# Two modulation products of layer 1 computed inside the norm between the layers

## The reference, cut to what matters

```python
def modulation(cond, w_mod, b_mod):            # w_mod: 1024 x 6144
    m = jax.nn.silu(cond) @ w_mod + b_mod
    return jnp.split(m[..., None, :], 6, axis=-1)

for l in range(2):
    mc, ml = modulation(c_ctx, ...), modulation(c, ...)      # context, latent
    hc, hl = modulate(xc, mc[0], mc[1]), modulate(xl, ml[0], ml[1])
    dc, dl = mixer(hc), mixer(hl)                # layer 1: pool_mixer
    x  = layer_norm(ALPHA * x + m[2] * d, ln1)   # m[2]: gate of the mixer
    f  = square(relu(modulate(x, m[3], m[4]) @ w_up)) @ w_down
    x  = layer_norm(ALPHA * x + m[5] * f, ln2)   # m[5]: gate of the MLP

def pool_mixer(h, p):
    u = h @ p["w_in"]                            # 1024 -> 1024
    pooled = multiscale_pool(u)                  # four windows, one per 256 channels
    mixed = einsum(pooled, pool_w) * pool_scale  # four 256x256 products
    return mixed @ p["w_out"]
```

## Time and profile before

| | us |
|---|---|
| median of 3 runs | 1475.55 |
| lowest, highest | 1473.79, 1476.63 |
| the profiled execution, its own time | 1473.62 |
| its span | 1471.8 |
| TensorE busy in it | 1405.8 (96%) |
| mean granted TensorE clock | 0.989 |

### The profile page before, as it was taken

One profiled execution on the slowest core, in us unless ns is written; L12 is line 12 of the kernel. 1 busy time (PEld: TensorE's weight loads), 2 busy tenths in 40 slices (PEclk: granted clock), 3 DMA queues, 4 the chain that ended last, 5 costly groups with the idle time before them and its releaser, 6 DMA issues.

```text
span 1471.8 us, 22812 instructions
## 1 busy us (share of the span) xinstructions
PE 1405.8 (96%) x8806; PEld 1245.6 (85%) x8806; DVE 1039.6 (71%) x1645; ACT 542.7 (37%) x976; POOL 79.1 (5%) x146
## 2 busy tenths in 40 slices
PE   4999999899999999999999999989999999999996
PEld 3899988666788998998899879868999899889985
DVE  3694566677468976776776796757797677667678
ACT  3333353267435432332233244434443233223322
POOL 1300000011200000000000010001000000000001
PEclk8999999999999999999999999999999999999998
DMA  9701233596713322322221523542332232123141
GB/s 317 220 29 59 87 117 129 167 342 209 249 57 114 130 84 61 115 79 65 85 92 58 208 77 129 186 148 76 121 125 84 62 111 85 59 85 98 59 172 72
DMA packets 132300, 177.47 MB, mean 121 GB/s; under 512 B 4170, under 2 KB 104258, under 8 KB 131698
## 3 DMA queue, kind: packets, MB, share of 16 engines
q1 hardware_dynamic: 123250, 146.46, 31.0%
q0 software_dynamic: 7376, 26.76, 5.3%
q10 hardware_dynamic: 1584, 3.01, 0.5%
HBM read 166.94 MB, written 9.27 MB: 120 GB/s over the span
## 4 chain that ended last, share of the span: by engine, by line
PE 80%; DVE 8%; ACT 5%; DMA 3%; issue 2%; ACTq 0%; POOL 0%; SPq 0%; DVEq 0%
PE ps L779 40%; PE ps L1288 20%; PE ps L761 7%; PE ps L770 4%; PE ps L810 2%; DVE convT L1992 2%; PE ps L1105 2%; ACT h_full L1688 1%; DVE wlo L1896 1%; DMA gate_parts<-modrow 1%; ACT whi L1398 1%; ACT tmp L1688 1%; PE ps L1116 1%; ACT e_att L1608 1%; DMA raw<-in_w_mod_l 1%
## 5 line engine op out<-in xcount | busy, mean ns | idle before, releaser
L1398 ACT ACTIVATE whi<-raw 128x512 fp32r<-128x512 f32 (+2 forms) x186 | 175.4, 953 | 357.1 <-PE ps L779 294.0
L779 PE MATMUL ps<-whi,hid_hi 128*128 128x512 f32 x640 | 249.6, 390 | 0.0
L779 PE MATMUL ps<-wlo,hid_hi 128*128 128x512 f32 x640 | 249.2, 389 | 0.0
L779 PE MATMUL ps<-whi,hid_lo 128*128 128x512 f32 x640 | 249.1, 389 | 0.0
L1896 DVE TENSOR_TENSOR wlo<-raw,whi 128x512 fp32r<-128x512 f32 (+2 forms) x186 | 201.7, 1093 | 24.4 <-ACT whi L1398 21.0
L779 PE MATMUL ps<-whi,h_hi 128*128 128x256 f32 (+1 forms) x480 | 158.7, 331 | 8.7 <-DVE h_lo L2696 5.4
L2325 DVE TENSOR_TENSOR acc<-acc,ps 128x512 f32<-128x512 f32 x120 | 80.3, 684 | 122.0 <-PE ps L779 122.0
L779 PE MATMUL ps<-whi,h_lo 128*128 128x256 f32 (+1 forms) x480 | 153.9, 321 | 0.0
L779 PE MATMUL ps<-wlo,h_hi 128*128 128x256 f32 (+1 forms) x480 | 153.7, 320 | 0.0
L779 PEld LDWEIGHTS ps<-whi,hid_hi 128*128 128x128 f32 x640 | 120.1, 188 | 25.3 <-DVE wlo L1896 0.8
L779 PEld LDWEIGHTS ps<-whi,hid_lo 128*128 128x128 f32 x640 | 120.1, 188 | 25.2
(11 more groups left out here) (337 smaller groups left out, 2669.9 us busy)
## 6 DMA issues: line engine op xcount, KB each, us to landing
raw<-in_w_up_l SPq DMA_DIRECT2D x32, 1024.0 KB, 5.6
raw<-in_w_down_l SPq DMA_DIRECT2D x32, 1024.0 KB, 5.1
raw<-in_w_mod_l SPq DMA_DIRECT2D x28, 1024.0 KB, 5.5
raw<-in_w_in_l SPq DMA_DIRECT2D x12, 1024.0 KB, 5.3
raw_split<-in_w_mod_l SPq DMA_DIRECT2D x8, 1024.0 KB, 6.9
raw<-in_w_out_l SPq DMA_DIRECT2D x5, 1024.0 KB, 6.2
x_spill<-x_tok POOLq DMA_DIRECT2D x10, 512.0 KB, 2.9
x_tok<-x_spill POOLq DMA_DIRECT2D x10, 512.0 KB, 6.0
```

What stands on the lines that cost most here:

```text
L779: mm = pe.matmul(out, a_of(still, k), w_of(part, k), start=(first and k == 0 and part == 0 and still == 0), stop=(last and k == nk - 1 and ...
L1398: act.activation(ring_piece(whi, w, g), piece(w, g), ACT.Copy).then_inc(hi_done, 1)
```

## The change

Products 40 and 41 (blocks 8 and 9 of layer 1) leave the loop of pool products and stand between `last_down(0)` and `first_units(1, ...)`. Their PSUM banks are 4 and 5, which groups 6 and 7 of the last down product used; PE waits for `acc_ok` 77 and 78 before them. Block 8 is loaded into slot 4 (the mixer's gate rows, no longer needed) ahead of w_in; block 9 into slot 2 (the first two accumulator tiles), once DVE has folded these into x (`acc_pre` 2), ahead of the second block of w_in. ACT copies the two rows after the second `split_hi` of the norm and stores them after the norm. The clearing of `ub` on POOL moves behind the norm, since block 9 lies in its place; `turn(1, 3)`, which writes banks 4 and 5, waits for both row copies.

The six products left (42 to 47) stand after the pool products f = 0, 1, 2, 3, 4 and 7. The stream has other places and other slots from there on.

```diff
 def weight_stream():
-            s += [("in", 1, BW * j) for j in range(4)] + [("pool", 1, 0)]
-            s += [("mod", 1, b) for b in (8, 9, 10, 11, 20)] + [("out", 1, 0)] + [("mod", 1, b) for b in (21, 22, 23)]
+            s += [("mod", 1, 8), ("in", 1, 0), ("mod", 1, 9)] + [("in", 1, BW * j) for j in range(1, 4)] + [("pool", 1, 0)]
+            s += [("mod", 1, b) for b in (10, 11, 20)] + [("out", 1, 0)] + [("mod", 1, b) for b in (21, 22, 23)]
...
-        OUT_SLOT = dict(zip(range(POOL_K + 1, POOL_K + 13), (3, 4, SOON, LATE, 3, 2, 4, SOON, LATE, 3, SOON, 2)))
+        MIX_K = mod_k[M_TAIL]
+        OUT_SLOT = dict(zip(range(MIX_K, MIX_K + 17), (4, 0, 2, 1, 0, 1, 0, 3, 4, 1, 2, 0, 3, 4, 1, 0, 2)))
...
         def tail_bank(m):
+            if m in (M_TAIL, M_TAIL + 1):
+                return 4 + m - M_TAIL
             return 6 if m > M_TAIL and m % 2 else 7
... SP, load
-                if k == POOL_K + 6:
+                if k == MIX_K + 2:
+                    sp.wait_ge(acc_pre[0], 2)
+                if k == w_k[W_OUT[1]]:
                     sp.wait_ge(pl_lo, KT)
... POOL
-            pool.memset(ub[:], 0.0).then_inc(zeros, 1)
             for g in range(2):
                 pool.dma_start(ic[:, g, :], ...)
             norm_share(1)
+            pool.wait_ge(mod_main, M_TAIL + 2)
+            pool.memset(ub[:], 0.0).then_inc(zeros, 1)
... PE, turn
+                if t == 3 and i == 1:
+                    pe.wait_ge(mod_row, M_TAIL + 2)
... PE, last_down
+                if layer == 0:
+                    for n in range(2):
+                        pe.wait_ge(acc_ok, DOWNS * layer + 77 + n)
+                        mod_product(M_TAIL + n)
... PE, loop of pool products
-                tail_mods(KT + f)
+                if f < 5 or f == 7:
+                    mod_product(M_TAIL + 2 + min(f, 5))
... ACT, last_norms
                 split_hi(w + 1)
+                if i == 1:
+                    mod_rows(M_TAIL)
+                    mod_rows(M_TAIL + 1)
                 normed(i, 3)
... ACT, after last_norms(1, W_IN1)
+            store_rows(M_TAIL)
+            store_rows(M_TAIL + 1)
... ACT, loop of pool products
-                tail_store(KT + f)
+                if 1 <= f < 6:
+                    store_rows(M_TAIL + 1 + f)
                 if f == 6:
                     split_hi(W_OUT[1])
-                tail_rows(KT + f)
+                if f < 5 or f == 7:
+                    mod_rows(M_TAIL + 2 + min(f, 5))
```

More of the change, by code:

```diff
@@ L363, in mlp_steps @@
                 yield kind, n, None
+        SITES = 32
+        M_TAIL = 8 + SITES
         THIRD_K = mod_k[22]
         POOL_K = w_k[W_IN1 + 4]
-        SOON, LATE = POOL_K % 2, (POOL_K + 1) % 2
-        OUT_SLOT = dict(zip(range(POOL_K + 1, POOL_K + 13), (3, 4, SOON, LATE, 3, 2, 4, SOON, LATE, 3, SOON, 2)))
+        MIX_K = mod_k[M_TAIL]
+        OUT_SLOT = dict(zip(range(MIX_K, MIX_K + 17), (4, 0, 2, 1, 0, 1, 0, 3, 4, 1, 2, 0, 3, 4, 1, 0, 2)))
         ATT_SLOT = dict(zip(range(THIRD_K, THIRD_K + 22), (2, 0, 1, 3, 4, 2, 0, 1, 3, 4, 2, 0, 1, 3, 4, 2, 0, 3, 4, 1, 0, 1)))
@@ L380, in raw_block @@
             if k >= FIRST_K and raw_slot(k) == 2:
-                return raw_pool[:] if k >= POOL_K else raw_att[:]
+                return raw_pool[:] if k in OUT_SLOT else raw_att[:]
             if k in ATT_SLOT and raw_slot(k) > 2:
@@ L488, in sums_of @@
             return 4 * (NS_UP * layer + u - SU)
-        SITES = 32
-        M_TAIL = 8 + SITES
         SKIP = 17
@@ L1350, in _ @@
             mlp(0)
[L1353 to L1356, removed]
             first_units(1, W_IN1, half_mm, u_mm)
@@ L1367, in _ @@
                         .then_inc(u_mm, 1)
-                    tail_mods(f)
             w = W_IN1 + 4
@@ L1838, in _ @@
                     split_hi(W_IN1 + (f + 3) // 2)
-                tail_rows(f)
             pool_high(KT - 1)
```

## The result

The changed kernel took 1477.85 us (median of 8 runs, 1476.51 to 1481.43) where the kernel before took 1474.67 (8 runs, 1472.25 to 1476.63). The medians are 3.2 us apart. The ratio estimated from all runs is 1.0028 (95% interval 1.0017 to 1.0039), which is 4.1 us slower, between 2.5 and 5.7. The forecast was 1.6 us faster. Its time lay in the range, its sign was wrong.

The account below looks back on a forecast made before the run. TensorE was taken as the bound, 80% of the chain. Norm +1.59, pool loop -0.35 and clock -2.88 summed to -1.64 us, taking 1475.55 to 1473.9 us; range 1470.8 to 1478.6.

Parts of the forecast that it names:

- Norm, +1.59: Layer 1's norm: the second moved product waits for DVE's read of group 7, so w_in starts 1.59 us late.
- ACT's freed work, -1.05: Pool loop: two row copies and one store leave ACT, gaining 1.05 us before w_out if block 21 is on time.
- Block 21, a stall of 4.1 us: Pool loop: block 21, landing in 8.4 us behind w_out's first block, keeps TensorE waiting 4.1 us after f = 3.
- the sum of this step, -0.35: Pool loop: with ACT's freed work and block 21's stall together, w_out starts 0.35 us earlier.
- The clock: Idle time before w_out: cut from 5.42 to 3.6 us, it no longer drops TensorE's clock; gain 2.88 us.
- the -2.88 of the sum: Start of w_out: 2.88 us gained on its first 48 matmuls because TensorE's clock stays up.
- a rival with a point at 4.3 us: Pool loop: TensorE's wait for block 21 reaches 4.3 us, its clock falls, costing 2.86; sum +2.0 or +4.9; 20%.
- Clock as it was: Before w_out: the clock still drops, or other runs did not lose it; sum +1.24, 1476.8 us; 17%.
- the late block: Pool loop: block 21 lands after 954.4 and the clock falls there; +2.0, 1477.6 us, or +4.9, 1480.4; 20%.
- the sum with both falls (+4.9): Clock falls in the pool loop and before w_out: +4.9 us, 1480.4; a third of a 20% case.

Follow-up runs that it names:

- Bank 3: The changed kernel with product 41 put in PSUM bank 3 in place of bank 5; 1474.78 us, ratio 1.0007.
- both costs mended: The changed kernel with product 41 in PSUM bank 3 and blocks 21 and 22 loaded ahead of w_out's first block; 1471.41 us, ratio 0.9979.
- the filled stall: The changed kernel with 14 matmuls of no use before product 45, where TensorE waits for block 21; 1477.00 us, ratio 1.0017.
- fillers: Useless matmuls in TensorE's idle time: 14 before product 45, changed kernel, 1477.00 us; 20 before w_out, kernel before, 1472.39; 14 there, mended kernel with spare rows, 1467.74.
- spare rows: Two extra row buffers so row copies don't wait for stores: in the kernel before, 1471.33 us; in the kernel with both costs mended, 1468.35 us.

## Why the prediction was wrong, step by step

**Norm, +1.59: right.** The second product ran at 877.30, 0.05 us behind the end of DVE's read of group 7 (876.56 + 0.69); 1.64 us reached the last w_in units. Bank 3 took it away. What hid the rest held too: ACT's two row copies and four stores lie in waits, and the transposes and units kept their distances.

**ACT's freed work, -1.05: right, but it showed only with the stream mended.** The kernel with both costs mended has 58.51 against 59.56. That it agrees to the digit is luck: from the scale of f = 5 on 8.50 us were left of 9.69, which is 1.19, and 0.14 were lost ahead of it. With block 21 alone moved up it was lost again to a store that landed later.

**Block 21, a stall of 4.1 us: right in kind, 3.42 by the landing of 7.8** (8.4 taken), and 4.63 by 9.0 in another execution. Two further kernels with the same stream had 8.3 and 8.4, so the 8.4 was well chosen. Without the clock the sum of this step, -0.35, holds as well: the filled stall gave -0.21. In the sum itself 0.2 us slipped: from the scale of f = 6 to w_out it was 7.05, less 0.45 for the store makes 6.6 and not 6.4. It measured 6.58 (965.99 to 972.57), and the step should have read about -0.2.

**The clock: the step that failed.** It was put as "at 3.6 I take it as held, because that is short of 4.3". The idle time before w_out was 4.03 us rather than 3.6, and the clock fell 3.1 us into it, where 3.6 would have met it too; so the -2.88 of the sum was not gained (+0.12). And the same reading left the clock up in the stall, which I made a rival with a point at 4.3 us. It fell at 2.8 us, in a stall of 3.42. From 955.24 to f = 5's start at 962.05 TensorE took 6.81 us, in the filled kernel 4.09 (958.20 to 962.29): 2.72 lost at the lower clock, near the 2.86 of that rival; less 0.64 by which the block came later in the filled kernel's loop this is the 2.1 between the two loops. That rival's sum was +2.0 with the fall in the loop alone and +4.9 with both; the case came out, with both, at +4.0 in the trace and +4.1 by the ratio (+3.2 by the medians). Of the 5.6 us between the forecast's -1.6 and the trace's +4.0, 3.0 lie at w_out's start and 2.2 in the loop.

What stands in place of "held below 4.3" is a tally of the twelve profiles, over all idle times of TensorE above 0.5 us from 60 us on, up to its last matmul:

| idle time, us | how many | the clock fell behind |
|---|---|---|
| 0.5 to 1.67 | 189 | 0 |
| 1.77 to 1.80 | 13 | 2 |
| 1.84 to 1.87 | 12 | 7 |
| 2.06 to 2.67 | 26 | 18 |
| 3.15 | 1 | 0 |
| 3.42 to 5.61 | 12 | 12 |

The falls came 1.9 to 5.2 us behind the last matmul ahead of the idle time, some of them when PE worked again. One row of one execution can't give the point at which the clock holds. And the trace of the kernel before had more than one row: its clock fell behind the 1.87 us at 1032.33, and behind 2.16 us at 366.51. Both are shorter than the 2.60 that stood for "left the clock up". The forecast had the doubt: the Trainium skill, TensorE: Matmul & The Clock Gate, Part 1, says that the monitor's window runs freely and that a kernel doesn't set its phase. The runs agree with it, by 7.28 against 8.80 us behind the same idle time of one kernel.

The doubt was weighed wrongly. Two idle times of 3.6 and 4.1 us had to keep the clock in most runs; with one observed fall at 4.3 and one hold at 2.60 that was no better than even for each, and both had to hold. "Clock as it was" and the late block together deserved more than 37%, and the sum with both falls (+4.9) no less than that with none.

**Left open.** What sets the moment of a fall. Whether it is the bunched loads that delay the row stores: the distance from a store's issue to the copy that waits for it was 5.57, 5.60 and 5.67 us in the three profiles with the stream of the kernel before, 5.63 to 6.29 in the four with the changed stream (6.29 being 948.50 to 954.79), 6.91 with block 21 moved up and 5.87 with both costs mended; a tendency, with the ranges overlapping. And how much of the medians' difference comes from unit 0: the kernel before dropped its clock there in 3 of the 4 executions with that idle time, the changed one in 1 of 4, too few for a rate. The same holds for the 1.5 us at the units of layer 1's MLP: the clock fell there in all seven traces without fillers or spare rows, and in none of the five with them. Whether those edits do that or chance isn't shown, so part of what they seem to gain may lie there.

## What to carry to other kernels

Where TensorE idles for some microseconds, price the clock behind it in each execution as a chance, and count a gain from a clock that "holds" only when the idle time is as short as ones that never dropped it (here 1.67 us). Before doing so, look through the whole trace, and not only the stretch that changes, for idle times of that length. Work moved earlier in one engine's program needs its loads moved in the queue as well; here a stall of 3.4 us was hidden by another engine's wait, and the clock that fell in it wasn't. And when work goes into an idle time, choose a buffer whose reader is done before that time begins: bank 3 instead of bank 5 was worth 1.6 us.

## What the runs showed of the hardware that I had not expected

- The clock can fall behind short idle times: behind the 1.84 to 1.87 us ahead of layer 1's MLP it fell in 7 of 12 executions, and behind 2.16 us at some 366 us in 10 of 12. Where it met two units of w_in or of the MLP, they took 8.8 us in place of 7.28.
- The clock can fall after TensorE has gone back to work: behind 3.91 us of idle time it fell 1.3 us after the next matmul had begun, and the 128x320 matmuls went from 0.46 to 0.73 us a pair.
- Fourteen to twenty matmuls of no use (3.4 to 4.8 us) in an idle time kept the granted clock at 1.00 in each of three kernels, and TensorE still waited 0.6 to 0.9 us behind them for what it needed.
- The second of two megabyte loads issued 0.4 us apart took 7.8 and 9.0 us in two executions of the same kernel, and 8.3 and 8.4 in two others with the same stream; that alone moved a stall from 3.42 to 4.63 us.
